# Latent layer of a four-layer trunk: a pair's rotary query units moved to the end of the even head's filling, staging one block earlier

## The reference

```
c_q, c_kv, k_rope, g = split(rmsnorm(x) @ w_in)      # 256, 128, 64, 2048 columns
q = (rmsnorm(c_q) @ w_uq)  -> 16 heads of 128 (nope) + 64 (rope)
q_rope = apply_rope(q_rope, cos, sin)                # x1*c - x2*s, x1*s + x2*c
k_nope, v = rmsnorm(c_kv) @ w_ukv                    # 16 heads of 128 + 128
k_rope = apply_rope(k_rope, cos, sin)                # one for all heads
for i in range(8):                                   # blocks of 128 queries
    s = (q_nope_i . k_nope + q_rope_i . k_rope) * scale, causal
    o_i = softmax(s) @ v
y = (o * silu(g)) @ w_out ;  x = x + y
```

## Time and profile before

| | us |
|---|---|
| median of 3 runs | 2728.34 |
| lowest and highest | 2726.56, 2731.05 |
| the profiled execution | 2728.8 |
| its span, first to last instruction | 2726.8 |
| TensorE busy | 2400.1 (88%) |
| VectorE busy | 1523.5 (56%) |
| ScalarE busy | 1325.1 (49%) |
| GpSimd busy | 358.5 (13%) |
| mean granted TensorE clock | 0.953 of full |

### The profile page before, as it was taken

The page is one execution under the profiler, slowest core; times in us unless marked ns, Lnnn a source line. Parts: engine busy times, 40 slices in busy tenths (PEclk is TensorE's granted clock), DMA queues, the critical chain, the costliest instruction groups (busy, mean ns, idle before and its releaser), DMA issues. The chain is left out here.

```text
span 2726.8 us, 42519 instructions
## 1 busy us (share of the span) xinstructions
PE 2400.1 (88%) x17068; PEld 1367.7 (50%) x17068; DVE 1523.5 (56%) x2164; ACT 1325.1 (49%) x1989; POOL 358.5 (13%) x266
## 2 busy tenths in 40 slices
PE   8999988977778878888787899999999899999987
PEld 4657753434444444444453455555554345775543
DVE  5555455665455455554556566666666474546554
ACT  4432333444444444444444477777777543334332
POOL 0000001121000000000002133222333210000001
PEclk9999999998889989999899999999999899999999
DMA  3011002213333332333332211111111121101013
GB/s 110 32 40 40 32 31 85 68 37 69 70 73 70 75 78 63 71 79 69 82 73 75 62 55 55 47 55 47 47 55 32 39 86 33 40 32 40 32 54 117
DMA packets 199767, 160.27 MB, mean 59 GB/s; under 512 B 160114, under 2 KB 165490, under 8 KB 199572
## 3 DMA queue, kind: packets, MB, share of 16 engines
q1 hardware_dynamic: 199572, 157.56, 21.7%
HBM read 98.79 MB, written 4.19 MB: 38 GB/s over the span
## 5 line engine op out<-in xcount | busy, mean ns | idle before, releaser
L222 PE MATMUL psum<-h_hi,w_hi 128*128 128x512 f16 x1128 | 431.6, 383 | 4.1 <-PEq L647 2.7
L223 PE MATMUL psum<-h_lo,w_hi 128*128 128x512 f16 x1128 | 431.1, 382 | 0.0
L224 PE MATMUL psum<-h_hi,w_lo 128*128 128x512 f16 x1128 | 430.7, 382 | 0.0
L2226 DVE SCALAR_TENSOR_TENSOR w_lo<-wf,w_hi 128x1024 f16<-128x1024 f32 (+3 forms) x194 | 232.3, 1200 | 188.8 <-ACT w_hi L2221 188.6
L238 PE MATMUL psum<-w_hi,h_hi 128*128 128x128 f16 x1504 | 256.9, 219 | 0.0
L239 PE MATMUL psum<-w_lo,h_hi 128*128 128x128 f16 x1504 | 256.6, 219 | 0.0
L240 PE MATMUL psum<-w_hi,h_lo 128*128 128x128 f16 x1504 | 256.6, 219 | 0.0
L1079 POOL TENSOR_TENSOR sb_al<-sb_zc,sb_ah 128x256 f16<-128x256 f32 (+2 forms) x96 | 166.3, 1732 | 372.0 <-ACT sb_ah L1044 372.0
L2221 ACT ACTIVATE w_hi<-wf 128x1024 f16<-128x1024 f32 (+3 forms) x194 | 188.4, 974 | 35.2 <-PE psum L224 16.3
L1578 ACT ACTIVATE ssum<-psum,mla_neg_top 128x128 f32<-128x128 f32 (+7 forms) x128 | 94.4, 738 | 207.7 <-DVE mla_neg_top L1487 207.7
L224 PEld LDWEIGHTS psum<-h_hi,w_lo 128*128 128x128 f16 x1128 | 111.2, 99 | 135.6 <-issue 4.7
(11 more groups left out here) (295 smaller groups left out, 5624.5 us busy)
## 6 DMA issues: line engine op xcount, KB each, us to landing
wf<-in_gla_out SPq DMA_DIRECT2D x32, 512.0 KB, 3.4
wf<-in_sb_in SPq DMA_DIRECT2D x32, 512.0 KB, 3.5
wf<-in_mla_out SPq DMA_DIRECT2D x20, 512.0 KB, 3.8
wf<-in_gla_v SPq DMA_DIRECT2D x16, 512.0 KB, 3.5
wf<-in_gla_g SPq DMA_DIRECT2D x16, 512.0 KB, 3.4
wf<-in_mla_gate SPq DMA_DIRECT2D x16, 512.0 KB, 3.5
wf<-in_sb_out SPq DMA_DIRECT2D x16, 512.0 KB, 3.5
xT<-in_x_T SPq DMA_DIRECT2D x16, 256.0 KB, 5.4
```

The lines of the kernel that those rows point to most:

```text
L222: pe.matmul(out, wh[:, w], act_hi[:, k, tok], start=(i == 0), stop=False)
L223: pe.matmul(out, wh[:, w], act_lo[:, k, tok], start=False, stop=False)
L224: mm = pe.matmul(out, wl[:, w], act_hi[:, k, tok], start=False, stop=(i == last))
L2226: dve.scalar_tensor_tensor(out=self.w_lo[s % Layer.NSPLIT][:, 0:cols], in0=self.wf[s % Layer.NLOAD][:, 0:cols], scalar=W_SCALE, in1=self.w ...
```

## The change

The filling of a head is now built by one function, `filling`, from up to four slabs, and a string sets the order of their units: six of the next head's projections, four of the output projection, two gates, two rotary units. The rotary slab and its two units are in the filling of the even head, as the last of it; `rope` stays in the odd head, now behind its second and third unit. The staging stands behind the halves of blocks 3 to 6 of the odd head instead of 4 to 7. All slabs from the fifth on are in `split_early`. Head 0 has the same units in the same order, with the `rope` items at the same units.

```diff
+    ORDER = "uuuuuuxxxxggrr", "uuuuuuxxxxggrr"
+    def add_units(self, slabs, order):
+        L, out, todo = self.L, [], []
+        for dram, cols, units in slabs:
+            todo.append((len(L.slabs), list(units)))
+            out.append(("w", len(L.slabs)))
+            L.slabs.append((dram, cols))
+        for i in order:
+            s, units = todo[i]
+            name, payload = units.pop(0)
+            out.append(L.add_unit(name, payload, s, self.ACC[len(L.units) % len(self.ACC)]))
...
-    def head_items(self, h):
-        out = []
-        if h % 2 == 0:
-            out += self.add_slab(self.w["q_rope"][h // 2], 256, [("qr", (h // 2, c)) for c in range(2)])
...
+    def filling(self, h):
+        made = {}
+        if h + 1 < MLA_HEADS:
+            made["u"] = self.up_slab(h + 1)
+        if h >= self.GROUP:
+            made["x"] = self.out_slab(h // self.GROUP - 1, h % self.GROUP)
+        if 1 <= h < MLA_HEADS - 1:
+            made["g"] = self.gate_slab(h + 1)
+        if h % 2 == 0 and h + 2 < MLA_HEADS:
+            made["r"] = self.rope_slab(h // 2 + 1)
+        turns = [k for k in self.ORDER[h % self.GROUP == 0] if k in made]
+        names = sorted(made, key=turns.index)
+        items = self.add_units([made[k] for k in names], [names.index(k) for k in turns])
+        if h % 2 and h + 1 < MLA_HEADS:
+            at = [i for i, it in enumerate(items) if it[0] == "u"][1:3]
+            for c, i in reversed(list(enumerate(at))):
+                items.insert(i + 1, ("rope", 3 + h + c))
+        return items
...
-        L.split_early = range(4, 7)
+        L.split_early = range(4, 1000)
...
-                if h + 1 < MLA_HEADS:
-                    filler += self.head_items(h + 1)
-                if h >= self.GROUP:
-                    filler += self.out_items(h // self.GROUP - 1, h % self.GROUP)
-                if 1 <= h < MLA_HEADS - 1:
-                    filler += self.gate_items(h + 1)
+                filler = self.filling(h)
...
-            if h % 2 and h + 1 < MLA_HEADS and 3 <= i < 7:
-                main += self.stage_items(h + 1, range(2 * i - 6, 2 * i - 4))
+            if h % 2 and h + 1 < MLA_HEADS and 2 <= i < 6:
+                main += self.stage_items(h + 1, range(2 * i - 4, 2 * i - 2))
```

More of the change, by code:

```diff
@@ L1202, in pe_cost @@
         return {"x": 12, "g": 24, "qn": 24, "kn": 12, "v": 12, "qr": 24}[name]
[L1205 to L1216, removed]
+    def add_units(self, slabs, order):
[8 more added lines that the diff above has]
+            out.append(L.add_unit(name, payload, s, self.ACC[len(L.units) % len(self.ACC)]))
+            n = out[-1][1]
+            if name == "x":
+                self.group_end[payload[3]] = n + 1
+            else:
+                self.unit[(name, *payload)] = n
             if name == "g":
@@ L1224, in add_slab @@
                 self.ropes.append((name[0], *payload))
-        return out + later
-    def gate_items(self, h):
-        return self.add_slab(self.w["gate"][h], 1024, [("g", (h, c)) for c in range(2)])
-    def head_items(self, h):
-        out = []
-        if h % 2 == 0:
-            out += self.add_slab(self.w["q_rope"][h // 2], 256, [("qr", (h // 2, c)) for c in range(2)])
[L1235 to L1240, removed]
-        return out
+        assert not any(units for _, units in todo)
@@ new lines, in add_units, with gate_slab, rope_slab, up_slab @@
+        return out
+    def gate_slab(self, h):
+        return self.w["gate"][h], 1024, [("g", (h, c)) for c in range(2)]
+    def rope_slab(self, p):
+        return self.w["q_rope"][p], 256, [("qr", (p, c)) for c in range(2)]
+    def up_slab(self, h):
+        return self.w["up"][h], 512, [(n, (h, c)) for n in ("qn", "kn", "v") for c in range(2)]
+    def out_slab(self, group, part, halves=range(2)):
+        final = group == MLA_HEADS // self.GROUP - 1
+        return self.w["out"][group * 4 + part], 1024, [("x", (2 * part + k, c, final, group)) for k in range(2)
+                                                       for c in halves]
@@ L1243, in stage_items @@
     def stage_items(self, h, quarters):
         return [("stage", 2 + h + i // 4, i % 4) for i in quarters]
[L1247 to L1252, removed]
     def build_items(self):
@@ L1259, in build_items @@
             self.unit[("c", *L.units[it[1]][1])] = it[1]
-        keys = self.add_slab(self.w["latent"][3], 1024, [("kr", (0, c)) for c in range(2)])
+        keys = self.add_units([(self.w["latent"][3], 1024, [("kr", (0, c)) for c in range(2)])], [0, 0])
         items = [("start",)] + first[0:4] + [("sums", 0), first[4], ("latent", 0), first[5]] + keys[:2]
         items += [("sums", 1)] + keys[2:] + [("latent", 1)]
-        items += self.gate_items(0) + [("rope", 0), ("rope", 1)]
-        items += self.head_items(0) + self.stage_items(0, range(8)) + self.gate_items(1)
-        L.split_early = range(4, 7)
+        items += self.add_units([self.gate_slab(0)], [0, 0]) + [("rope", 0), ("rope", 1)]
+        own = self.add_units([self.rope_slab(0), self.up_slab(0)], [0, 0] + [1] * 6)
+        items += own[:5] + [("rope", 2)] + own[5:6] + [("rope", 3)] + own[6:] + self.stage_items(0, range(8))
+        items += self.add_units([self.gate_slab(1)], [0, 0])
+        L.split_early = range(4, 1000)
         last = MLA_HEADS * TT - 1
@@ L1290, in build_items @@
             for part in range(4):
[L1291 removed]
+                tail += self.add_units([self.out_slab(MLA_HEADS // self.GROUP - 1, part, (c,))], [0, 0])
         early, tail = L.open_early(L.cut(tail, ("x",)), 3)
```

2 lines of the change are left out of this document (removed).

## The result

The changed kernel takes 2696.48 us (median of 4 runs, 2695.64 to 2702.71); the kernel before, run beside it, 2729.03 us (2726.56 to 2731.05). The ratio is 0.9886, 95% interval 0.9869 to 0.9903: 32.5 us faster. The forecast was 2671 us in a range of 2645 to 2700, so the time lies inside the range, near its slow end, and of the 57.5 us forecast little more than half came.

What follows compares the result with a forecast made beforehand. TensorE was taken to bound the kernel, with 20 us of waiting per 112.5 us pair of heads. Staging 34 + 11, rotary move 13 + 4, less 4.5 at the start, gave 57.5 us: 2671 us, range 2645 to 2700.

Steps and rivals of the forecast that it cites:

- layer's start: First staging of the latent layer, behind a slab load that waits for its split: 4.5 us lost, 2 to 7.
- heads 0 to 3: First four heads: 11 us from staging into heads 2 and 4, 4 us from rotary units into heads 1 and 3.
- heads 4 to 13, five pairs: Steady heads: 34 us from staging into even heads, 13 us from moving rotary units away from odd heads' front.
- the staging: Rotary query copies one block earlier: 6.8 us at each of five even seams, 34 us, plus 11 into heads 2 and 4.
- The rotary move: Rotary units moved to the even head's end: 2.6 us at each of five odd seams, 13 us, plus 4 us earlier.
- the early splits: Slabs split as soon as their buffer is free: costed at nothing, removed low-half waits counted with staging and rotary move.
- Into an even head: Seam from product to first output projection: 17.3 us against 24.1, staged wait 3.5 us instead of 8.3.
- The granted clock, left half open: Even seam: low clock cost about 1.4 us; whether it falls in a 3.5 us wait left open, 0.7 us counted.
- Into an odd head: Seam from product of block 53 (T) to first output projection: 25.8 us against 29.9, counted as 2.6 us gained.
- the first rival: Odd seam: VectorE's two rotary groups cost the waits they remove; even seams win only 4.8 us each; 2698 us; 15%.
- Into heads 1 and 3: Early odd seams: moving the rotary units gains 2 us each, 4 us, with the softmax chain as limit.
- the early splits make it slower: Rival: about 44 early-split slabs delay the softmax, 101 us lost against 57.5 won, 2772 us; 5%.

Runs made afterwards that it cites:

- e1: Kernel before with only the staging copies one block earlier, behind blocks 3 to 6 of the odd head: 2690.3 us, ratio 0.9856.
- e4: Changed kernel with the staging copies put back behind blocks 4 to 7 of the odd head: 2741.3 us, ratio 1.0048.
- after: The changed kernel itself, with the whole change, against the kernel before: 2696.5 us, ratio 0.9886.
- e10: Changed kernel with a gate's steps that stood between a block's maximum and its halves moved behind the halves: 2680.0 us, ratio 0.9824.
- e3: Changed kernel with the two `rope` items one unit earlier, behind the odd head's first and second query unit: 2684.8 us, ratio 0.9838.
- e2: Changed kernel with the early slab splits limited to slabs 4 to 6 again: 2706.9 us, ratio 0.9920.
- e8: Kernel before with staging one block earlier and the early slab splits, rotary units not moved: 2676.5 us, ratio 0.9817.
- e5: Changed kernel with `rope` items one unit earlier and rotary units in the middle of the even head's output projection: 2670.4 us, ratio 0.9790.

## Why the prediction was right and where it was wrong

The gain taken apart by the starts of the even heads' first scores, before and after (600.08 and 603.14, 792.57 and 790.71, 1356.42 and 1322.13, then the ends of the spans):

| term | forecast | measured |
|---|---|---|
| layer's start | -4.5 | -3.1 |
| heads 0 to 3 | 11 + 4 | 4.9 |
| heads 4 to 13, five pairs | 34 + 13 | 32.4 |
| heads 14 and 15, and the rest | 0 | -2.7 |
| sum | 57.5 | 31.6 (span) |

By edits instead of stretches: the staging was forecast at 34 + 11 = 45 us and is worth 40 (e1) and 45 us (e4). The rotary move and the early splits together were forecast to give 13 + 4 - 4.5 = 12.5 us and cost 0.30% or 8 us (0.9856 in e1, 0.9886 in after), the rotary move with its later `rope` items losing 17 to 19 and the splits, whose gain the forecast did not count apart, winning 9 to 11. So it is the staging that put the time inside the range.

**Into an even head: right in each step.** (T is the product of block 61.) Staged was laid out at T+7.3 and came at 7.34; the wait 3.5 us, measured 3.59; from product to output projection 17.3 us, measured 17.3. That the gate's steps precede the halves, which this rests on, e10 showed. The granted clock, left half open, fell: 0.54 in the 3 us behind the wait, so the lower of its two levels for nearly all of them. "TensorE: Matmul & The Clock Gate" in the Trainium skill, section "What's actually happening", knows two levels, the lower as the default. The row of 0.54 behind 3.59 us of idleness agrees. Even so the stretch came out as forecast, since the bank wait of 1.58 us went entirely where I had left 0.3.

**Into an odd head: the step that failed.** The first half came as laid out: a wait of 4.1 us at the first key unit at T+12.1 became 3.97 us at T+11.94. The step that failed is the end of the layout: "the second value unit behind the key's low (18.4, waits 1.6), the first output projection behind the second key's low, at 22.1 (waits 3.0)", with its ground given in the first rival: "the 4.7 us came from GpSimd's and ScalarE's queues, which are free now". GpSimd's was not free. I had laid out VectorE, ScalarE and TensorE instruction by instruction and left GpSimd out, and in it the second rotary sum stands behind y_lo. The output projection started at T+24.05 and waited 4.87 us. e3 moved that sum ahead of y_lo, with the rounding and the low half that go with it, and took 2.77 us off the wait and 2.8 us off the head. The gain, reckoned over the whole stretch from the product of block 53 to that of block 61, is 58.75 against 56.27 us, 2.5 us, with 12 matmuls (2.6 us) fewer standing in it, which is none; the forecast was 2.6 us, five times. Part of it went behind the waits, where the granted clock was 0.50 for 3 us and 0.53 for 5 us.

So five pairs gave 6.5 us each where 9.4 were forecast: 6.8 from the even seam and nothing from the odd one. The windows confirm it from the other side: TensorE's idle time in a pair fell by 7.1 us and its busy time rose by 0.8.

**Heads 0 to 3: the staging's part right, the rotary part of the wrong sign.** 15 us were forecast, 11 from the staging and 2 us each for heads 1 and 3; 4.9 came. The waits of 10.4 and 10.1 us for the staged queries fell to 3.35 and 4.75 us, by 12.4 us, where I had counted 11. On the kernel before, the same staging brought 12.7 us in these heads (192.5 to 179.8 in e1). The step that failed is "Into heads 1 and 3 I take 2 us each, 4 us, as less stands there for VectorE": with the rotary units moved these four heads are 8.9 (e1 to e2) and 7.4 us (e8 to after) longer. What grows is the wait for turnings, 31.7 us in after, the longest 5.21, where it was 21.2 before and 20.3 in e1. The sentence goes on to name the softmax chain as the limit there, and I counted a gain all the same. By which step the moved units delay that chain was not tested.

**The start: -3.1 for -4.5.** The cause was as laid out (e2 has no wait there), and the copies were done at 601.4 and not 602.5.

**The end: -2.7 us, not forecast.** At the seam into head 14 the first output projection comes 13.3 us behind the first scores, with the wait of 1.58 us still in it, where the seams before have 10.0 us and none; it was 12.0 us. Why this seam differs I did not test, and it stays open. The other 1.4 us lie in the rest of head 14 and behind it: from the first scores of head 15 to the end of the span it is 1324.9 us before and 1326.1 after, and the ten experiments spread over 1324.8 to 1328.7, so most of that is within the scatter of single traces.

**The rivals.** The first, "the rotary work takes over", gave 2698 us and came nearest by its number and by its account of the odd seam: the rotary groups cost what the waits removed gave. e3, e8 and e5 make it sharper: most of that cost was the later `rope` items, the even head's end is without them about as good a place for the units as the old one, and the middle of the filling is a better one. Its other half, that into an even head only 4.8 us are won, was wrong; 6.8 were. That the early splits make it slower was wrong in sign: they give 9 to 11 us (e2, e8). I gave this first rival 15% and the forecast 65%; a layout with one queue missing did not earn the difference.

## What to carry to other kernels

Lay out every in-order queue that the moved work passes through, also the one that is busy 13% of the time: here a wait of 4.9 us in TensorE came from GpSimd, whose only part was to hold an addition behind a step that waited for ScalarE. A staging that is late is mended by its place in the issuing queue (one block gave 40 us here), and once the wait is small, what counts is what delays the transposition ahead of it. Look at the front of a layer apart from its steady part: the whole lead of e1 over the change lay in the start and the first four heads. Where several small edits at one seam have been told apart, put together those that win: the change as a whole won 32 us, its parts, placed anew, 84.

## What the runs showed of the hardware

- The granted clock is at 0.54, 0.50 and 0.53 for 3, 3 and 5 us behind waits of 3.59, 3.97 and 4.87 us, and at 0.50 behind 8.33 us: a wait of half the length costs the clock all the same, and halving a wait does not give back what the clock takes. Behind the wait of 0.79 us in e1 it stayed at full:

```profile
992.90:995.90 3.00, 3.00 (x35) 2.17 (x36) 2.24 (x5) 1.16 (x3) 0.00 (x0) 1.00 0.88 48
```

- GpSimd's rotary sum of 128x512 takes 1.26 us by itself (961.61 in after) and longer where a VectorE instruction with two inputs from SBUF, the on-chip memory, begins 0.05 us ahead of it: 1.77 us beside one of 0.69 us, and 2.30 us beside the slab's low half of 1.23 us (e3, shown above). In both it ends 1.12 to 1.13 us behind VectorE's instruction, so that it looks as if it began only then. Beside a maximum of 1.09 us that VectorE reads from PSUM it takes 1.26 us. In after, then in e3:

```profile
947.35 0.69 DVE L290 TENSOR_TENSOR mla_silu_g<-mla_silu_g,mla_gate_tmp 128x512 f32<-128x512 f32 x1
947.40 1.77 POOL L1641 TENSOR_TENSOR mla_rt<-mla_rt 128x512 f32<-128x512 f32 x1 [16.48 <-DVE mla_rt L1475]
```
```profile
632.14 1.09 DVE L1497 TENSOR_REDUCE mla_top<-psum 128x1 f32<-128x896 f32 x1
632.19 1.26 POOL L1641 TENSOR_TENSOR mla_rt<-mla_rt 128x512 f32<-128x512 f32 x1 [7.05 <-DVE mla_rt L1475]
```

  The Trainium skill, "SBUF — State Buffer", section "SBUF: two separate sides", says that the two engines share a pair of ports which one of them holds for a whole instruction and the other waits for. These rows agree, though no experiment varied them on purpose.
